# Thirteen of the 22 column-block pairs of a gated MLP's up projection by seven half products in place of eight

## The reference

```python
def conv_gated_mlp(x, w_up, conv_w, w_down):
    h = causal_dwconv(x @ w_up, conv_w)      # w_up 1024 x 5632, three taps along the tokens
    gt, val = jnp.split(h, 2, axis=-1)
    return (jax.nn.silu(gt) * val) @ w_down  # w_down 2816 x 1024
```

## Time and profile before

| | us |
|---|---|
| median of 3 runs (lowest to highest) | 1194.71 (1192.77 to 1196.61) |
| time of the profiled execution | 1193.91 |
| its span in the profile | 1192.2 |
| TensorE busy in the span | 1143.3 (96%) |
| up projection, stretch of the chain from 710.43 | 308.58 |
| down projection, stretch of the chain from 1019.01 | 146.47 |

### The profile page before, as it was taken

One profiled execution on the slowest core, in us unless ns is written; L12 is line 12 of the kernel. 1 busy time (PEld: TensorE's weight loads), 2 busy tenths in 40 slices (PEclk: granted clock), 3 DMA queues, 4 the chain that ended last, 5 costly groups with the idle time before them and its releaser, 6 DMA issues.

```text
span 1192.2 us, 22860 instructions
## 1 busy us (share of the span) xinstructions
PE 1143.3 (96%) x9511; PEld 945.3 (79%) x9530; DVE 704.4 (59%) x982; ACT 565.9 (47%) x1053; POOL 367.0 (31%) x378
## 2 busy tenths in 40 slices
PE   5999999899999999999988999999999999999996
PEld 5788879788887877878767878888888888888885
DVE  5788976656678776867546734333333333655744
ACT  7444332457555555565565644333333334445443
POOL 2477346223031121121231025455555444200000
PEclk9999999999999999999998999999999999999998
DMA  8245120500000000000124453222222221653651
GB/s 253 73 124 171 72 51 20 116 28 23 2 23 21 2 23 21 3 2 2 38 60 157 159 155 89 71 71 71 71 71 75 80 75 53 242 164 124 230 193 71
DMA packets 104078, 99.86 MB, mean 84 GB/s; under 512 B 15412, under 2 KB 89384, under 8 KB 103976
## 3 DMA queue, kind: packets, MB, share of 16 engines
q1 hardware_dynamic: 102536, 93.15, 25.5%
q10 hardware_dynamic: 1440, 5.24, 1.1%
HBM read 85.24 MB, written 13.11 MB: 82 GB/s over the span
## 4 chain that ended last, share of the span: by engine, by line
PE 86%; DVE 7%; ACT 3%; DMA 1%; issue 1%; SPq 1%; POOL 0%; ACTq 0%; DVEq 0%
PE psum L1697 26%; PE psum L1980 14%; PE psum L2516 9%; PE psum L1344 8%; PE psum L1591 5%; PE psum L1524 4%; PE psum L2556 4%; PE psum L1540 4%; PE psum L1505 3%; DVE arena L2403 2%; PE psum L1337 1%; PE psum L1289 1%; PE psum L1271 1%; PE psum L1425 1%; PE psum L1407 1%
## 5 line engine op out<-in xcount | busy, mean ns | idle before, releaser
L1697 PE MATMUL psum<-h_p,up_p 128*128 128x512 f32 x704 | 221.1, 390 | 1.2 <-DVE arena L1673 0.7
L1697 PE MATMUL psum<-h_q,up_q 128*128 128x512 f32 x704 | 220.8, 389 | 0.0
L1814 DVE SCALAR_TENSOR_TENSOR arena<-psum,arena 128x1023 f32<-128x1023 f32 x44 | 56.4, 1283 | 196.1 <-ACT arena L1783 196.1
L1763 POOL TENSOR_TENSOR up_q<-arena,up_p 128x1024 fp32r<-128x1024 f32 x44 | 105.9, 2407 | 212.0 <-ACT up_p L1759 212.0
L1697 PEld LDWEIGHTS psum<-h_p,up_p 128*128 128x128 f32 x704 | 132.2, 188 | 29.3 <-POOL up_q L1763 1.1
L1697 PEld LDWEIGHTS psum<-h_q,up_q 128*128 128x128 f32 x704 | 132.2, 188 | 27.3
L1783 ACT ACTIVATE arena<-psum,arena 128x1024 f32<-128x1024 f32 x44 | 49.1, 1117 | 199.0 <-PE psum L1697 199.0
L1344 PE MATMUL psum<-arena 64*64 64x64 f32 x3072 | 110.8, 221 | 2.6 <-DVE arena L1120 1.5
L1980 PE MATMUL psum<-dn_p,ap_p 128*128 128x512 f32 x352 | 110.2, 394 | 3.2 <-DVE ap_q L1873 3.2
L1344 PEld LDWEIGHTS psum<-arena 64*64 64x64 f32 x3072 | 97.5, 135 | 17.8 <-issue 6.8
L1980 PE MATMUL psum<-dn_q,ap_q 128*128 128x512 f32 x352 | 109.9, 394 | 0.0
(11 more groups left out here) (299 smaller groups left out, 2150.9 us busy)
## 6 DMA issues: line engine op xcount, KB each, us to landing
arena<-in_ffn_w_up SPq DMA_DIRECT2D x44, 512.0 KB, 3.9
arena<-in_ffn_w_down SPq DMA_DIRECT2D x44, 512.0 KB, 3.7
arena<-in_w_in SPq DMA_DIRECT2D x20, 512.0 KB, 3.9
arena<-in_x SPq DMA_DIRECT2D x16, 512.0 KB, 5.5
qkv_mid<-arena ACTq DMA_DIRECT2D x9, 512.0 KB
arena<-qkv_mid SPq DMA_DIRECT2D x8, 576.0 KB, 4.3
arena<-in_w_out SPq DMA_DIRECT2D x8, 512.0 KB, 3.8
x_mid<-arena SPq DMA_DIRECT2D x8, 512.0 KB, 3.3
```

Of the source, the lines that this page charges most:

```text
L1697: ins = pe.matmul(up_ps[j % 2][:, g, h * 512:(h + 1) * 512], w[:, k], x[:, k, h * 512:(h + 1) * 512], start=k == 0 and x is h2_p, stop=Tru ...
L1763: pool.tensor_tensor(up_q[up_slot(u)], up_st[up_slot(u)], up_p[up_slot(u)], ALU.subtract).then_inc(late("up_lo")[0], 1)
L1814: v.scalar_tensor_tensor(out=y[:, 1:S], in0=ps[:, 0:S - 1], scalar=tap(1, u), in1=y[:, 1:S], op0=ALU.mult, op1=ALU.add).then_inc(late("up_ ...
```

## The change

Pairs 0 to 2 stay as they are. The other 19 run by the pattern c s s, c s s, ... and end with s s s. A pair marked "c" (3, 6, 9, 12, 15, 18) is made with eight half products as before, in four steps a1, a2, b1, b2 of 16 matmuls. A pair marked "s" (13 of them) is made with the seven products of Strassen's scheme in Winograd's form, each of 8 matmuls. I write 6.7 for product 6 of pair 7; products run in the order 1 5 6 2 7 4 3, and the first product of the next pair goes between 7 and 4.

The tokens' four operand sums (`t_p`, `t_q`) are made once at the start on VectorE and ScalarE. For every "s" pair VectorE makes four sums of half weight blocks (L2151 of the new program), each product has its own hi split (`slab_p`, ring of five, L1992) and lo split on GpSimd, and products 1, 6, 7 and 4 follow each other in one PSUM bank: after 1, 6 and 7 ScalarE copies the bank out (L2056), and the next of them waits for the copy. VectorE adds three copies back in PSUM (L2158). Product 3 waits for the second of those adds. Taps (L2012), the other taps (L2112, L2115) and SiLU (L2048) stay; the gated product moves from GpSimd to VectorE (L2163), and the gate goes through one buffer `y_a` for all pairs, so that the gate tap of a pair waits for the product of the pair before. The gated products of pairs 3 to 20 go to HBM (`act_mid`, 512 KB each) and come back in halves of 256 KB in the down projection. A planner (`up_steps`) gives each step a time in units of one product, and each engine runs its steps sorted by that time. The down projection's own loop is unchanged, but its first splits are among the planned steps.

```diff
+CLASSIC = 3
+RING = 5
+UP_KINDS = "csscsscsscsscsscsss"
+SEVEN = [j for j in range(CLASSIC, NF) if UP_KINDS[j - CLASSIC] == "s"]
...
+        if j in SEVEN:
+            own = [(i, j) for i in (1, 5, 6, 2, 7, 4, 3)]
+        else:
+            own = [(i, j) for i in (A1, A2, B1, B2)]
+        if j - 1 in SEVEN:
+            order.insert(len(order) - 2, own.pop(0))
+        order += own
+    return order
+
+
...
+    hi = {m: at(end[MULTS[n - RING]] if n >= RING else n - 4.5, "hi", *m) for n, m in enumerate(MULTS)}
+    lo = {m: at(hi[m] + 0.4, "lo", *m) for m in MULTS}
+    prod = 0
+    for j in range(CLASSIC, NF):
+        if j in SEVEN:
+            s1 = at(hi[5, j] - 0.9, "sum", 5, j)
+            s2 = at(max(s1 + 0.1, hi[6, j] - 0.6), "sum", 6, j)
+            s3 = at(max(s2 + 0.1, hi[7, j] - 0.6), "sum", 7, j)
+            s4 = at(max(s3 + 0.1, hi[3, j] - 0.6, lo[5, j] + 0.8), "sum", 3, j)
+            for i in (1, 6, 7):
+                at(end[i, j] - 0.05, "copy", i, j)
+            at(end[2, j] + 0.05, "add", 2, j)
+            c22 = at(end[7, j] + 0.45, "add", 5, j)
+            c12 = at(end[3, j] + 0.05, "add", 3, j)
+            tap_b = at(max(end[4, j], c22 + 0.4) + 0.02, "tap", 1, j)
+            conv_b = at(max(tap_b + 0.65, c12 + 0.05), "conv", 1, j)
+            tap_a = at(max(c12 + 0.4, tap_b + 0.1, prod + 0.7), "tap", 0, j)
+            conv_a = at(max(tap_a + 0.65, conv_b + 1.4), "conv", 0, j)
+            free = max(lo[4, j], lo[3, j], lo[7, j], s4) + 0.7
+        else:
+            tap_a = at(max(end[A2, j], prod + 0.7), "tap", 0, j)
+            conv_a = at(tap_a + 0.65, "conv", 0, j)
+            tap_b = at(end[B2, j], "tap", 1, j)
+            conv_b = at(max(tap_b + 0.65, conv_a + 1.4), "conv", 1, j)
+            free = lo[B2, j] + 0.7
+        silu = at(conv_a + 1.45, "silu", j)
+        prod = at(max(silu + 0.6, conv_b + 1.4), "prod", j)
+        if j < NF - 1:
+            at(prod + 1.0, "spill", j)
+        if j + 2 < NF:
...
+    for kk, time in ((0, -5.0), (2, -3.5), (1, -3.4)):
+        at(down(time), "dn_load", kk)
+    for kk, first, rows in ((0, -2.5, -1.9), (1, -0.9, -0.8), (2, 0.75, 0.8)):
+        at(down(first), "dn_hi", kk)
+        at(down(first + 0.5), "dn_lo", kk)
+        at(down(rows), "ap_hi", kk)
+        if kk < 2:
+            at(down(rows + 0.4), "ap_lo", kk)
+    return [step for _, step in sorted(steps, key=lambda x: x[0])]
...
+        def up_run(steps):
+
+            for step in UP_STEPS:
+                if step[0] in steps:
+                    steps[step[0]](*step[1:])
...
+        def spill(sp, j):
+            sp.wait_ge(*late("up_prod", j + 1))
+            sp.dma_start(act_mid[j], y_b[j % 2]).then_inc(late(f"act_st{j % 2}")[0], 16)
...
+            def dn_load(kk):
+                if kk == 0:
+                    part_done(sp, 3, NF - 2)
+                elif kk == 2:
+                    mult_done(sp, 1, NF - 1)
+                else:
+                    sp.wait_ge(*late("up_mm", 2 * CLASSIC + max(n for n in range(PRODUCTS) if n % RING == 3) + 1))
+                down_load(sp, kk)
...
+        def split_mult_hi(act, i, j):
+            n = mult_at(i, j)
+            if n >= RING:
+                act.wait_ge(*late("up_mm", 2 * CLASSIC + n - RING + 1))
...
+            if i in (3, 5, 6, 7):
+                sum_done(act, i, j)
+            else:
+                pair_landed(act, j)
+            act.activation(slab_p[n % RING], part_source(i, j), ACT.Copy, scale=1.0 - SPLIT_W).then_inc(late("up_hi")[0], 1)
+
+        def split_mult_lo(pool, i, j):
+            n = mult_at(i, j)
+            pool.wait_ge(*late("up_hi", 2 * CLASSIC + n + 1))
+            pool.tensor_tensor(slab_q[n % RING], part_source(i, j), slab_p[n % RING], ALU.subtract).then_inc(late("up_lo")[0], 1)
...
+            def tap_(g, j):
+                if j in SEVEN:
+                    for i in ((2, 3), (5,))[g]:
+                        add_done(act, i, j)
+                    mult_done(act, (3, 4)[g], j)
                 else:
...
+                    mult_done(act, (A2, B2)[g], j)
...
+                if g == 0:
+                    act.wait_ge(*late("up_prod", j))
+                elif j >= CLASSIC + 2:
+                    spilled(act, j - 2)
...
+            def silu(j):
+                conv_done(act, 0, j)
+                act.activation(y_of(0, j), y_of(0, j), ACT.Silu).then_inc(late("up_silu")[0], 1)
+
+            def copied(i, j):
+
+                mult_done(act, i, j)
+                before = max((x for x in SEVEN if x < j), default=None)
+                if before is not None:
+                    add_done(act, {1: 2, 6: 3, 7: 5}[i], before)
+                act.activation(u_s[i], mult_ps(i, j), ACT.Copy).then_inc(late("c_cp")[0], 1)
...
+            def weight_sum(i, j):
+                if i == 5:
+                    pair_landed(v, j)
...
+                elif i == 6:
+                    sum_done(v, 5, j)
+                    out, x, y, op = s_e2[j % 2], s_e1[j % 2], w_of(j, 0, 0), ALU.subtract
...
+            def added(i, j):
+
+                mult_done(v, i, j)
+                copy_done(v, {2: 1, 5: 7, 3: 6}[i], j)
+                out = c_ps(1, j)[:, right] if i == 5 else mult_ps(i, j)
+                v.tensor_tensor(out, mult_ps(i, j), u_s[{2: 1, 5: 7, 3: 6}[i]], ALU.add).then_inc(late("c_add")[0], 1)
...
                     pe.wait_ge(*late("up_conv", u - 3))
                 up_products(pe, u, (1,) if u < 3 else (0, 1)).then_inc(late("up_mm")[0], 1)
+
+            for n, (i, j) in enumerate(MULTS):
+                pe.wait_ge(*late("up_lo", 2 * CLASSIC + n + 1))
+                if i in (1, B1):
+                    conv_done(pe, 1, j - 2)
+                if i in (2, 5, A1):
+                    conv_done(pe, 0, j - 2)
+                if j < CLASSIC + 2 and i in (1, 2, 5, A1, B1):
+                    conv_done(pe, 1, j - 2)
+                if i in (5, 7):
+                    pe.wait_ge(*late("t_lo", 2))
+                if i in (6, 7):
+                    copy_done(pe, {6: 1, 7: 6}[i], j)
+                if i == 4:
+                    copy_done(pe, 7, j)
+                    pe.wait_ge(*late("t_lo", 4))
+                if i == 3:
+                    add_done(pe, 5, j)
+                for k in range(HT):
+                    if j in SEVEN:
+                        for w, x in ((slab_p[n % RING], x_p[i]), (slab_q[n % RING], x_q[i])):
+                            ins = pe.matmul(mult_ps(i, j), w[:, k], x[:, k], start=k == 0 and x is x_p[i] and i in (1, 2, 5),
+                                            stop=True, skip_group_check=True)
...
+            elif kk == 1:
+                act.wait_ge(*late("up_mm", 2 * CLASSIC + max(n for n in range(PRODUCTS) if n % RING == 4) + 1))
...
+        def act_reload(sp, kk):
+            m, k = divmod(kk, NF)
...
+            sp.dma_start(act_rows(kk), act_mid[k][:, HT * P * m:HT * P * (m + 1)]).then_inc(sem(f"act_ld{n % 4}"), 16)
...
+            mult_done(sp, 4, NF - 1)
+            down_load(sp, 3)
+            for j in range(CLASSIC, NF - 1):
+                spilled(sp, j)
+            sp.wait_ge(*late("up_mm", 2 * CLASSIC + PRODUCTS))
+            add_done(sp, 3, NF - 1)
+            for kk in RELOADS[:3]:
+                act_reload(sp, kk)
...
-                                pe.wait_ge(*late("up_conv", NU - HT + 1 + t))
+                                conv_done(pe, 1 - t % 2, NF - 2 + t // 2)
```

336 lines of the change are left out of this document (272 added, 64 removed).

## The result

The changed kernel took **1216.31 us** (1212.83 to 1216.71) against 1193.93 for the kernel before on the same chip: a ratio of **1.0178, 95% interval 1.015 to 1.0206**. One execution each of the changed kernel (1283.34 us, granted clock 0.84) and of e6_small_pool (2203.6 us) was slow; ranges and ratios are of the others, whose medians are 1215.9 and 1214.42, while the times given are medians of all. The forecast was 1199.0 with a range of 1184 to 1209: slower was right, but the time is 17 us over the forecast and 7 over the range. The profiled execution took 1216.71 us, its span is 1215.0, 22.8 us over that of before.

The account below looks back on a forecast made before the run. The prediction took TensorE's matmuls as the bound. Against the profiled 1193.9 us: - 23.6 removed + 9.7 + 1.0 + 11.2 of stalls + 6.0 of clock = 1198.2, median 1199.0 us; range 1184 to 1209 for 8 in 10.

Parts of the forecast that it names:

- Removed, 23.6 us: Up projection: thirteen "s" pairs save 104 matmuls of 0.227 us each, 23.6 us.
- Place A: Products 6.7, 6.10, 6.13, 6.16, 6.19: a 16.4 us chain against 14.5 us of TensorE, 1.9 us each, 9.7 in all.
- Place B: Products a1.6 to a1.18: TensorE waits for gate taps, 0.2 us at each of five places, 1.0 in all.
- Place C: Last three pairs and down projection's start: 0.5 before 4.20, 0.8 before 3.20, 2.1 at 4.21, 7.7 before tile 2; 11.2 us.
- The clock: TensorE's clock falls behind stalls, 1.7 us each: 3.5 falls, two of them at the five 1.9 us stalls, 6.0 us.
- Rival 3: Stalls come as forecast, but short ones leave the clock alone: 1194.7 us, no change; chance 0.22.
- Without cost: Start, pairs 0 to 2: seven operand sums and four splits among the taps, covered by 36 us of TensorE; no cost.
- Rival 4: VectorE is the bound through its port shared with GpSimd, its SBUF instructions waiting for full splits: 1209 us; chance 0.19.
- Spills and reloads: 18 x 512 KB each way to HBM, at no cost; if cover is gone, 1 to 3 us at two places.

Follow-up runs that it names:

- e6_small_pool: Changed kernel with three quarters of GpSimd's low splits left out in the pairs from 3 on: 1214.73 us.
- e2_place_a: Changed kernel with ScalarE making value tap and copy behind product 1 ahead of high split 7 and SiLU in five pairs: 1197.55 us.
- e12_best3: Changed kernel with reordered start, five places and last pair, swapped down-weight blocks, pair 2's gated product on VectorE, no work left out: 1179.2 us, 0.9881 of the kernel before.
- e10_half_silu: Changed kernel with half of the SiLU of the pairs with eight products left out: 1206.85 us.
- e1_small_sums: Changed kernel with three quarters of the operand sums left out (512 of 2048 columns made), every instruction still issued: 1200.45 us.
- e5_half_place_a: Changed kernel with only the copy behind product 1 moved ahead of the previous pair's SiLU, still behind the tap, at five places: 1205.22 us.
- e3: Changed kernel with the places of down-weight blocks 1 and 2 exchanged, so block 1 can load earlier: 1211.39 us.
- e4: Changed kernel with the start reordered on ScalarE, GpSimd and VectorE and the first two products' ring places shifted, all sums made: 1207.5 us.
- e7_all: Changed kernel with the start order, five-place order and down-weight swap together, plus two moves in the last pair: 1188.04 us.
- e8_all_start2: e7_all with two weight sums of pair 4 ahead of pair 2's last convolutions and a low split ahead of pair 1's gated product: 1186.4 us.

## Why the prediction was right and wrong, point by point

- **Removed, 23.6 us: right.** In e2_place_a 1096 matmuls fill 251 us without a gap, 0.229 each; in e12_best3, 1193.9 - 23.6 + 3.5 (two waits of the start) + 1.7 (a fall) + 2.9 (0.73, 0.77, 1.43 at the end) = 1178.4, measured 1179.2.
- **Place A, 1.9 us five times: right to 0.05 us**, released by the copy, through the chain as it was laid out. **Place B, 0.2 each: nothing was seen.** Place C: 7.7 us at tile 2 (7.71) right and 2.1 at 4.21 (1.72) nearly; of the 0.5 before 4.20 there were 0.2, of the 0.8 before 3.20 nothing.
- **The clock: mechanism right, number short.** "I take two of five" was four of five, and 6.0 us in all were 8.2 at place A alone. By e2_place_a the place cost 18.8 us where the sum had 9.7 + 3.4. Rival 3, that short waits leave the clock alone, falls for 1.95 us; for waits of 1.5 us at the same places it held in all five (e10_half_silu).
- **"Without cost", the start: this is the step that failed.** The prediction counted seven operand sums, priced them by what each may wait for GpSimd, set that against 36 us of TensorE, and never multiplied the instructions by their own length. There are twelve (eight sums and four low parts): 12 x 2.28 = 27.4 us of VectorE, 42.7 with the six pairs of taps (2 x 1.28 each), and high parts of 1.92 on ScalarE ahead of taps and splits. It also looked at the port from one side: VectorE's eleven instructions took 7.1 us more beside GpSimd, and GpSimd's products and splits, for which TensorE waited, up to 2.0 us more each. Nor did the splits of pair 3 need only the pair's weights: those at 755.19 waited 7.27 us on ScalarE for the eighth sum. The step cost 15.9 us (e1_small_sums), nearly the whole miss of 17.
- **Rival 4, the port: wrong for the pairs that it was written for** (e6_small_pool). It stretched sums by 16.7 us in all, off the path. At the start, where the prediction had only VectorE wait for GpSimd, it is on the path in both directions; its share of the 15.9 us is not shown.
- **Spills and reloads at no cost: right.** The down projection's chain behind tile 2 is 146.76 us for 632 matmuls, against 146.47 for 640 before.

The bill, from the undone parts: - 23.6 + 15.9 (start) + 18.8 (place A) + 12.2 (the end: 7.7 + 1.7 idle and 2.8 of slow clock in the windows 1040 to 1050) = + 23.3 us; measured + 22.4. Each of the undone parts is good to some 3 us, so that the sum closes no better than that.

## What to carry to other kernels

Work that is "made once at the start" still has an engine and a length: multiply count by duration, add it to what that engine does there already, and compare with what TensorE has, before asking who waits for whom. In queues that run in order, look for an instruction that waits at the head for data while a ready one, on which TensorE depends, stands behind it; moving two steps gave back 18.8 us here. And before adding up the gains of single edits, look in each profile for a second place that the edit touched: one gain was counted twice here. Before moving an instruction that "nobody needs yet", look for every wait on it in the code.

## What the runs showed of the hardware

- Single waits of TensorE of 0.78 to 1.72 us had no fall of the clock behind them in 19 cases (0.78 and five times 1.00 in e5_half_place_a, five times 1.51 or 1.52 in e10_half_silu, and product 4.21's 1.68 to 1.72 in these two, the changed kernel, e1, e2, e3, e4 and e6). Waits of 1.93 to 1.95 us had one in 19 of 26 (after, e1, e3, e4, e6), though program and wait were the same each time, and the wait of 2.15 to 2.17 us at 723.5 in three of six (after, e2, e3; not e5, e6, e10). Two waits close together are another case: in e7_all 1.54 us stood 2.7 us behind a wait of 1.13, and the clock was 0.50 from 1014 to 1016; in e8_all_start2, with 1.14 and 1.54, it stayed at 1.00. At place A, shortening a wait from 1.95 to 1.51 us brought the next such product 0.4 us earlier where no fall had stood behind it and 2.0 us where one had.
- A fall is free where another engine sets the end: behind 743.60 the clock stayed at 1.00 in the changed kernel and fell to 0.59 in e2_place_a (745 to 750), and the next product started at 756.29 and 756.51 all the same; the idle time before it was 5.11 and 2.71. The row at 743.5 to 743.8 shows the price as well: its wait was 3.62 to 3.66 us in the three kernels with a fall behind 723.5 and 5.25 or 5.26 in the three without, so the fall had cost TensorE 1.6 us, and nothing came later by it.
- GpSimd's split of 512 columns took 1.45 us on average in the up projection (median 1.30, at most 3.31, beside a VectorE instruction of 2048 columns), and the same split of 128 columns 0.54.
